# Narrow input-projection columns on four column groups, query forget sums added in the mask pass, past suffix sums moved ahead: one hybrid decoder layer step

## What is computed

```python
qa, ka, va, ra, lra, qb, kb, vb, fb, ga, gb = jnp.split(h @ w_in, offs, axis=-1)
log_a = jax.nn.log_sigmoid(lra @ w_a2 + b_a) / 16        # lra: 16 columns of w_in
logf = jax.nn.log_sigmoid(fb + b_f)                       # fb: 8 columns, one per attention head
# prompt attention, per head, F = cumsum(logf)
s = einsum('bqhd,bkhd->bhqk', q, k) * scale + F[query] - F[key]
p = softmax(where(query >= key, s, -inf)); o = p @ v
# sample attention over 1024 paged past rows: R = suffix sums of the past rows' logf (exclusive)
R = cumsum(lf_past, reverse=True) - lf_past
s_past = q @ k_past * scale + Fn[..., None] + R
```

## Time and profile before

| | |
|---|---|
| time, median of 3 runs | 1935.51 us (1934.56 to 1939.46) |
| the profiled execution's span | 1934.0 us |
| its own device time | not listed; the span is 0.6 us under the fastest run |
| TensorE busy | 1767.3 us (91%), 11144 records |
| VectorE, ScalarE, GpSimd busy | 534.1 (28%), 210.8 (11%), 156.1 us (8%) |
| chain that ended last, by engine | PE 65%, issue 12%, DMA 10%, DVE 5% |
| moved | 531.09 MB, mean 275 GB/s |

### The profile page before, as it was taken

The page is one execution under the profiler, slowest core; times in us unless marked ns, Lnnn a source line. Parts: engine busy times, 40 slices in busy tenths (PEclk is TensorE's granted clock), DMA queues, the critical chain, the costliest instruction groups (busy, mean ns, idle before and its releaser), DMA issues.

```text
span 1934.0 us, 27785 instructions
## 1 busy us (share of the span) xinstructions
PE 1767.3 (91%) x11144; PEld 1114.0 (58%) x11144; DVE 534.1 (28%) x1152; ACT 210.8 (11%) x405; POOL 156.1 (8%) x274
## 2 busy tenths in 40 slices
PE   7799999999998999978889999997699998998998
PEld 4366666666666877756667777775333333333335
DVE  3100000000047744455553111003323222231233
ACT  2010000000001201102222100002110001000002
POOL 1011111111110001410000000000100000000000
PEclk9899999999999999988899999998799899999999
DMA  9997887677516335538999874242499999999992
GB/s 371 402 380 273 317 297 285 246 262 289 198 49 201 100 111 168 207 119 298 385 392 368 325 271 134 88 174 94 146 368 406 397 397 384 410 404 383 401 391 96
DMA packets 154570, 531.09 MB, mean 275 GB/s; under 512 B 17701, under 2 KB 61899, under 8 KB 131803
## 3 DMA queue, kind: packets, MB, share of 16 engines
q1 hardware_dynamic: 128834, 432.24, 58.9%
q0 software_dynamic: 17088, 97.15, 14.1%
q10 hardware_dynamic: 8578, 0.73, 0.4%
HBM read 510.94 MB, written 19.15 MB: 274 GB/s over the span
## 4 chain that ended last, share of the span: by engine, by line
PE 65%; issue 12%; DMA 10%; DVE 5%; SPq 4%; DVEq 1%; POOL 1%; ACT 1%; POOLq 1%; ACTq 0%; PEldq 0%
PE ps L652 62%; DMA ring<-in_w_up_e_dram 4%; DMA ring<-in_w_ada_dram 2%; PE ps L662 2%; SPq L399 2%; DMA xT<-in_w_ada_dram 2%; SPq L393 2%; DMA xT<-in_w_in_dram 2%; POOL work L537 1%; DVE z L1468 1%; DVE z L1459 1%; DVEq L2115 1%; DVE ring L1465 1%; POOLq L536 0%; DVE ring L1837 0%
## 5 line engine op out<-in xcount | busy, mean ns | idle before, releaser
L652 PE MATMUL ps<-hT,ring 128*128 128x288 f32 x2304 | 585.3, 410 | 5.3 <-PE ps L652 3.6
L652 PEld LDWEIGHTS ps<-hT,ring 128*128 128x128 f32 x2304 | 430.0, 190 | 169.7 <-issue 59.1
L652 PE MATMUL ps<-ring,work 128*64 128x512 f32 (+1 forms) x1280 | 273.4, 617 | 25.3 <-DMA ring<-in_w_ada_dram 12.2
L652 PE MATMUL ps<-z,ring 128*128 128x288 f32 (+1 forms) x1040 | 255.5, 407 | 4.5 <-PE ps L652 2.7
L1468 DVE COPY z<-ps 128x256 f32<-128x256 f32 (+7 forms) x98 | 64.3, 660 | 677.1 <-PE ps L652 656.9
L652 PE MATMUL ps<-ring,z 32*32 32x256 f32 (+3 forms) x3744 | 213.9, 396 | 21.2 <-DVE z L1468 11.2
L652 PEld LDWEIGHTS ps<-z,ring 128*128 128x128 f32 x1040 | 196.4, 190 | 62.8 <-issue 7.5
L652 PEld LDWEIGHTS ps<-ring,work 128*64 128x64 f32 (+1 forms) x1280 | 77.8, 134 | 181.4 <-issue 165.7
L652 PEld LDWEIGHTS ps<-ring,z 32*32 32x32 f32 (+3 forms) x3744 | 108.5, 114 | 115.2 <-issue 108.3
L1263 ACT ACTIVATE z<-ps 128x512 f32<-128x512 f32 (+4 forms) x108 | 60.1, 602 | 860.3 <-PE ps L652 850.4
L1465 DVE SCALAR_TENSOR_TENSOR xT<-ps,modT,xT 128x256 f32<-128x256 f32 x160 | 70.8, 480 | 254.3 <-PE ps L652 254.2
(11 more groups left out here) (209 smaller groups left out, 877.4 us busy)
## 6 DMA issues: line engine op xcount, KB each, us to landing
ring<-in_w_in_dram SPq DMA_DIRECT2D x36, 2048.0 KB, 14.3
ring<-in_w_gate_e_dram SPq DMA_DIRECT2D x32, 2048.0 KB, 12.7
ring<-in_w_up_e_dram SPq DMA_DIRECT2D x32, 2048.0 KB, 18.4
ring<-in_w_down_e_dram SPq DMA_DIRECT2D x32, 2048.0 KB, 15.0
ring<-in_w_ada_dram SPq DMA_DIRECT2D x16, 2048.0 KB, 20.5
z<-in_w_ada_dram POOLq DMA_DIRECT2D x32, 1024.0 KB, 7.9
xT<-in_w_ada_dram POOLq DMA_DIRECT2D x32, 1024.0 KB, 6.7
ring<-in_cache_v_dram SPq DMA_DIRECT2D x64, 512.0 KB, 5.8
```

What stands on the lines that cost most here:

```text
L652: return nc.tensor.matmul(o, lhsT, rhs, start=start, stop=stop, skip_group_check=free)
```

## The change

Three edits. First, the 24 narrow columns of `w_small` become 32 wide (lra at 0, fb at 16, zeros behind), and the 16 products go on the four column groups of the array in turn, K tile k to group k % 4, so four partial sums stand in the four quarters of PSUM's rows. VectorE copies all 128 rows to SBUF (`small_parts`, in `ms`), and one more product with a matrix of zeros and ones (`small_fold`, built from `ident` at the start) adds the quarters and puts the rows where they stood before. Four gate products move from the 56 to the place between the two. Second, in the prompt attention the two products with `fT` go; instead TensorE turns the forget sums once, VectorE copies them (`f_tok`, one column per block and head), and the mask pass becomes two operations, one per query block, that add that column and a mask in one go; for the second block the mask is 256 wide, its first half zeros (`mask_two`). Third, VectorE's copy and sums of the past's log-forgets move ahead of the small products' copy and so of both log-sigmoids.

```diff
-        w_small = work2[:, 2048:2048 + KT * 40].rearrange("p (k n) -> p k n", n=40)
+        w_small = work2[:, 2048:2048 + KT * 32].rearrange("p (k n) -> p k n", n=32)
+        small_fold = work2[:, 2048 + KT * 32:2048 + KT * 32 + 40]
+        small_parts = ms[:, :]
...
+        f_tok = w3[:, 4000:4016].rearrange("p (q h) -> p q h", q=2)
+        mask_two = w3[:, 4020:4020 + 2 * P]
...
             for k in range(KT):
-                last = mm(ps[0:40, 6, 0:T], w_small[:, k, :], hT[:, k, :], k == 0, k == KT - 1)
-            last.then_inc(reach("lra_fb_ready"), 1)
+                g = k % 4
+                last = mm(ps[32 * g:32 * g + 32, 6, 0:T], w_small[:, k, :], hT[:, k, :], k < 4, k >= KT - 4)
+            last.then_inc(reach("small_summed"), 1)
...
+            gates(4)
+            pe.wait_ge(*step("small_copied"))
+            mm(ps[0:40, 6, 0:T], small_fold, small_parts, True, True).then_inc(reach("lra_fb_ready"), 1)
             gates(8)
...
-            gates(56)
+            gates(52)
...
             pe.wait_ge(*step("f_ready"))
             pe.wait_ge(sem("tok_copied"), 4)
+            for q in range(2):
+                last = tr(ps[:, 3, q * H_B:(q + 1) * H_B], fT[:, q * P:(q + 1) * P])
+            last.then_inc(reach("f_turned"), 1)
...
                         mm(o, qb[:, h, q * P:(q + 1) * P], kb[:, h, 0:kk], True, False)
-                        mm(o, hot.to_broadcast([H_B, P]), nfT[:, 0:kk], False, False)
-                        last = mm(o, fT[:, q * P:(q + 1) * P], hot.to_broadcast([H_B, kk]), False, True)
+                        last = mm(o, hot.to_broadcast([H_B, P]), nfT[:, 0:kk], False, True)
...
+                    if h == 0:
+                        pe.wait_ge(*step("f_tok_copied"))
...
-            act.dma_start(w_small[:, :, 32:40], io["w_in"][0, :, COL_FB:COL_FB + 8].rearrange("(k p) n -> p k n", p=P)).then_inc(sem("w_small_loaded"), 16)
+            act.dma_start(w_small[:, :, 16:24], io["w_in"][0, :, COL_FB:COL_FB + 8].rearrange("(k p) n -> p k n", p=P)).then_inc(sem("w_small_loaded"), 16)
...
             tt(fold, ident[:, 0:64], ident[:, 64:P], ALU.add)
+            v.wait_ge(sem("w_small_clear"), 1)
+            nc.vector.memset(small_fold, 0.0)
+            v.drain()
+            by_group = ident[:, :].rearrange("p (g i) -> p i g", g=4)
+            nc.vector.tensor_reduce(small_fold[:, 0:16], by_group[:, 0:16, :], AX.X, ALU.add)
+            nc.vector.tensor_reduce(small_fold[:, 32:40], by_group[:, 16:24, :], AX.X, ALU.add)
...
+            v.wait_ge(sem("lf_loaded"), 16 * DB * NPG)
+            copy(lf_p, lf_in.rearrange("p b n h -> p h b n"))
+            v.drain()
+            nc.vector.memset(lf_b[:, :, :, NPG - 1], 0.0)
+            v.drain()
+            for n in range(NPG - 2, -1, -1):
+                tt(lf_b[:, :, :, n], lf_b[:, :, :, n + 1], lf_p[:, :, :, n + 1], ALU.add)
+                v.drain()
+            v.sem_inc(reach("forgets_ready"), 1)
+            v.wait_ge(*step("small_summed"))
+            copy(small_parts, ps[:, 6, 0:T]).then_inc(reach("small_copied"), 1)
             v.wait_ge(*step("lra_fb_ready"))
...
             log_sigmoid(laf, buf[0], buf[1], buf[2], buf[3], "za", 1.0 / 16)
-            v.wait_ge(sem("lf_loaded"), 16 * DB * NPG)
...
-            v.sem_inc(reach("forgets_ready"), 1)
             log_sigmoid(fT[:, :], ms[0:H_B, :], fa, fb_, fc, "zf", 1.0)
...
             v.sem_inc(reach("f_ready"), 1)
+            nc.vector.memset(mask_two[:, 0:P], 0.0)
+            copy(mask_two[:, P:2 * P], fox_mask[:, :])
+            v.wait_ge(*step("f_turned"))
+            copy(f_tok, ps[:, 3, 0:2 * H_B].rearrange("p (q h) -> p q h", q=2))
+            v.drain()
+            v.sem_inc(reach("f_tok_copied"), 1)
...
-                    diag = ps[:, 1 + h % 2, :].rearrange("p (n q) -> p n q", q=P)[:, 0:3:2, :]
-                    tt(diag, diag, fox_mask[:, :].unsqueeze(1).to_broadcast([P, 2, P]), ALU.add)
+                    for q, mask in ((0, fox_mask[:, :]), (1, mask_two)):
+                        o = ps[:, 1 + h % 2, q * P:q * P + P * (q + 1)]
+                        stt(o, o, f_tok[:, q, h:h + 1], mask, ALU.add, ALU.add)
```

More of the change, by code:

```diff
@@ L53 @@
     "pe_step": (
-        "c_turned ss1_ready vec_turned lra_fb_ready za_ready past_summed va_turned kt_turned state1_ready "
-        "oa_ready update2_ready os_own_ready os_state_ready os_turned ss_a_ready lf_turned "
+        "c_turned ss1_ready vec_turned small_summed lra_fb_ready za_ready past_summed va_turned kt_turned state1_ready "
+        "oa_ready update2_ready os_own_ready os_state_ready os_turned ss_a_ready lf_turned f_turned "
         "s_new_ready o_all_turned ss2_ready raw_logits logits_ready rank_ready lists_summed").split(),
@@ L60 @@
     "dve_step": (
-        "c_silu cT_ready ms1_ready lra_copied za_read forgets_ready logf_ready past_ready va_copied decay_rel "
+        "c_silu cT_ready ms1_ready forgets_ready small_copied lra_copied za_read logf_ready past_ready va_copied decay_rel "
         "decayed_ready kt_copied state1_copied oa_copied gla_prompt_ready update2_used os_summed "
         "gla_sample_ready os_turned_copied ms_a_ready rs_a_ready rs_a_inverted "
-        "kv_tok_ready gla_scratch_free f_ready s_new_copied ob_ready work_free ms2_ready logits_copied member_ready pos_ready "
+        "kv_tok_ready gla_scratch_free f_ready f_tok_copied s_new_copied ob_ready work_free ms2_ready logits_copied member_ready pos_ready "
         "table_ready list_ready").split(),
```

## The result

The changed kernel took **1922.42 us** (median of 4 runs, 1918.79 to 1930.64) against 1935.65 for the kernel before beside it (4 runs): a ratio of 0.9933, 95% interval 0.9907 to 0.9958. That is 13.2 us faster, by more than the 0.3% that a measurement can tell. The forecast was 1916.4, inside a range of 1912.5 to 1924.5. The sign was right, and about a third of the forecast gain did not come. The profiled execution is the slowest of the four runs.

What follows compares the result with a forecast made beforehand. TensorE was taken to bound the level products and prompt attention, DMA from 880 to 1055 us. 14.3 us (5.0 + 6.6 + 2.7) plus 4.8 made 19.1: 1935.5 to 1916.4 us; own range 1914.2 to 1919, stated 1912.5 to 1924.5.

Steps and rivals of the forecast that it cites:

- Narrow columns: Small products ahead of the gates: 7.88 us becomes 2.1, the fold adds 0.8, net 5.0 us of TensorE.
- that rival: Small products: column groups take turns, products keep 7.88 us, gain 13.3 in all, kernel 1922.2; chance 0.04.
- some tenths: Before the fold: four gate products on TensorE and VectorE's copy to SBUF end within some tenths of a us.
- Suffix sums: Past pages' sums moved ahead: the 6.59 us TensorE wait goes whole, and the clock staying up gives 1.8 and 0.9 more.
- the page rows: Wait ahead of VectorE's stage: 64 row loads done by about 540, before 547.2; rival that they land late, chance 0.02.
- VectorE late next: At the copy of the turned values: VectorE ready 1.0 us ahead of TensorE's 14.3; rival that its chain takes over, 0.08.
- Forget sums in the mask pass: Prompt attention, eight heads: 6.6 of products saved, less 0.4 transposes and VectorE's added time, gives 4.8 us.
- the second bill: After the 6.59 us wait for the suffix sums: granted clock 0.50, then 0.83 on average over the next 5.6 us.
- The rival that had all heads go by VectorE: Prompt attention: VectorE's chain sets every head, -3.0 us in place of +4.8, kernel 1924.2; chance 0.10.
- the 6.6 for the products: Prompt attention: two 8-row products per head go, 0.31 + 0.52 = 0.83 us, 6.6 for eight heads.
- The other sum given there, 5.1: Attention gain if VectorE's two mask operations cost +0.26 us a head by its 0.96 GHz, instead of +0.33.
- What passes it on: First page load of the busy DMA stretch, at 855.74, moves with TensorE to near 837; no loss counted through later stages.

Runs made afterwards that it cites:

- the first profile of after: First profiled execution of the changed kernel, the slowest of its four runs; median 1922.42 us against 1935.65 for the kernel before.
- the split: Changed kernel with GpSimd's 128x2304 product issued as eight of 128x288, the rest as changed: 1916.47 us, ratio 0.99 against the kernel before.

## Why the prediction was right, and where it was not

**Narrow columns: right.** The products took 2.08 us (2.1 forecast); the groups do not take turns, so that rival falls. The fold took 0.61 us to the next start and began 0.16 us later than four gate products at the usual pace (0.4925) would let it, within the "some tenths" that were given. The net is 7.88 - 2.08 - 0.61 - 0.16 = 5.0, as forecast.

**Suffix sums: right.** The wait went whole, the clock stayed up, the page rows were no hindrance. Alone it was worth 8.95 us in the trace. That the two parts need each other follows from VectorE's chain, and the wait of 8.54 us with the narrow columns alone shows it.

**VectorE late next: right.** 1.0 us of slack was forecast and 1.72 is left, so its chain did not take over. The two parts were 14.3 on paper and 13.95 in the trace.

**Forget sums in the mask pass: the step that failed** is "In three heads TensorE already waits, 2.6 us in total, and each loses 0.33", and with it the 4.8 us. The price on VectorE was right, 0.32 us more. But two of the three waits were no matter of VectorE's mask pass. The last head's, 1.24 us, has no scores beside it and stayed at 1.25. In the other, VectorE's scaling was held by GpSimd's product, whose place does not move when a head gets shorter; so TensorE's wait grew by what TensorE gained, from 1.21 to 2.42 and 2.58 us, and not by 0.33. Behind that, in both profiles of the changed kernel, came some 10 us of half clock, and that head took 11.26 and 11.29 us instead of 6.57. This is the second bill that the prediction had itself read from the earlier trace rows for the other wait and did not ask for here. The attention came out 0.6 to 1.1 us longer where 4.8 less was forecast. The rival that had all heads go by VectorE gave 1924.2, near the result, but for a reason that the clean heads and the split refute.

A term was mis-sized beside it: the 6.6 for the products. It read 0.83 us a head from the starts, and 0.65 left it, 5.2 in eight heads, since the products that stay hold TensorE longer. A clean head won 0.62 and not 0.83 - 0.08 = 0.75. The other sum given there, 5.1, does not follow from its terms either: with 0.26 in place of 0.33 they come to 6.6 - 0.4 - 3 x 0.26 - 5 x 0.01 = 5.4.

With the product in pieces the edit gives 3.8 us in the profiles and 6.1 in the medians, and the kernel 1916.47, the number forecast for the change as it stood. That this number came is partly luck. By the profiles its gain of 19.3 us from the first small product to the first page product is 13.95 for the first two parts, some 1.4 for the old wait that they take away and some 4.0 for the heads, where 14.3, nothing and 4.8 were forecast. The measured 1922.42 is outside the forecast's own range, which ended at 1919; it lies in the stated one because that had been drawn out to 1924.5.

**What passes it on: right as far as the page load.** The first page load of the busy stretch came at 845.69 in the first profile of after and not near 837, by what the attention lost and that execution's later start. In the split kernel, where the heads do win, it comes at 836.52. The stages behind it differ by up to 6 us between executions of one kernel, as the table shows, and no loss there can be put down to the change.

**What stays open.** The profiles tell the pause from the clock. With neither the three columns are 242.9 (split), with a pause of 2.64 or 2.68 us alone 244.9 and 244.8, with the half clock behind it 249.4 and 248.9: some 2 us for the pause and 4 for the clock. What decides whether the clock falls is not shown: it did behind 2.42 and 2.58 us, it did not behind 2.64 and 2.68, and at the first head of two kernels it did with no wait at all. How many of the executions that were not profiled have it, and so how much of each median it makes, is not shown either.

## What to carry to other kernels

When TensorE waits for another engine, ask first what that engine itself was doing. A VectorE operation that took four to six times its usual length beside a long GpSimd instruction was held here, and its wait changed with the order of things, not with the work in it. Cutting that GpSimd instruction into pieces was worth 4 to 6 us in this kernel, though GpSimd itself needed 1.06 us more; it is the thing to try in a like case. Work moved to cover a wait leaves a gap where it came from: here the clock fell there. And when two edits each look worth little alone, look for the wait that they share: the narrow columns needed the moved sums, and the shorter heads needed the split.

## What the runs showed of the hardware

VectorE's scaling of SBUF values was held to the end of the GpSimd instruction that ran: 0.55 us became 3.10, 3.26 and 2.34 behind a product of 5.05 us, and 1.66 behind pieces of about 0.8. Its operations on PSUM beside the same product were not held (0.36, 0.48 and 0.62 us, as elsewhere). Eight pieces took 6.10 us where the whole took 5.04.

The granted clock after a pause is not the same in every execution: 0.50 for some 10 us behind waits of 2.42 and 2.58 us, and 1.00 throughout behind 2.64 and 2.68. It was 0.52 over 7.1 us behind a stretch in which TensorE did not wait.

Two VectorE operations of 0.36 and 0.48 us with no dependence between them start 0.27 us apart, so the pair took 0.75 us, not 0.84.
